# One decoder layer on one core: the sums of the layer input on GpSimd, the rotary key's tile in two passes, the conditioning shared out anew

## The reference, cut to what matters

```python
mod = jax.nn.silu(c) @ w_ada[l] + b_ada[l]
shift, scale, gate = jnp.split(mod[:, None, :], 3, axis=-1)
h = rmsnorm(x, g_pre[l]) * (1.0 + scale) + shift
proj = h @ w_in[l]                      # 1024 x 9920 columns
# c_q 384, c_kv 256, k_pe 64, then gates, retention q, k, v, merge gates
y_mla = mla_branch(c_q, c_kv, k_pe, positions, ...)   # k_pe gets a rotary turn
y_ret = retention_branch(...)
x = x + gate * (merged @ w_out[l])
return rmsnorm(x, g_final)
```

## Time and profile before

| what | us |
|---|---|
| median of 3 runs | 1617.9 |
| the runs | 1614.6, 1617.9, 1619.55 |
| span of the profiled execution | 1616.2 |
| TensorE busy | 1568.4 (97% of the span) |
| VectorE busy | 959.4 (59%) |
| ScalarE busy | 605.1 (37%) |
| GpSimd busy | 322.0 (20%) |

### The profile page before, as it was taken

The page is one execution under the profiler, slowest core; times in us unless marked ns, Lnnn a source line. Parts: engine busy times, 40 slices in busy tenths (PEclk is TensorE's granted clock), DMA queues, the critical chain, the costliest instruction groups (busy, mean ns, idle before and its releaser), DMA issues. The chain is left out here.

```text
span 1616.2 us, 20288 instructions
## 1 busy us (share of the span) xinstructions
PE 1568.4 (97%) x7568; PEld 1308.9 (81%) x7568; DVE 959.4 (59%) x1626; ACT 605.1 (37%) x1057; POOL 322.0 (20%) x280
## 2 busy tenths in 40 slices
PE   5999999999999999999999999899999999999998
PEld 4778888888888888798888888787688888888886
DVE  6984444444444457752566665567987775647544
ACT  5444333333333343342343433334544443213111
POOL 2232223322322200200000000015655530000000
PEclk9999999999999999999999999999999999999999
DMA  9132332223323334799265554447977767345422
GB/s 385 38 130 105 111 112 110 107 109 115 120 104 111 95 97 164 301 414 322 82 209 170 181 184 164 179 137 260 323 235 228 250 204 281 115 137 183 143 105 78
DMA packets 142225, 278.70 MB, mean 172 GB/s; under 512 B 11056, under 2 KB 83632, under 8 KB 133552
## 3 DMA queue, kind: packets, MB, share of 16 engines
q1 hardware_dynamic: 125488, 245.09, 43.6%
q10 hardware_dynamic: 12032, 15.54, 2.9%
q0 software_dynamic: 4608, 16.78, 2.7%
HBM read 182.47 MB, written 94.37 MB: 171 GB/s over the span
## 5 line engine op out<-in xcount | busy, mean ns | idle before, releaser
L1579 DVE TENSOR_TENSOR w_form<-w_pair,w_form 128x512 fp32r<-128x512 f32 x150 | 116.3, 776 | 127.2 <-ACT w_form L1211 125.6
L1211 ACT ACTIVATE w_form<-w_pair 128x512 fp32r<-128x512 f32 x150 | 94.6, 632 | 245.3 <-PE p_banks L2093 237.2
L2090 PE MATMUL p_banks<-h_hi,w_form 128*128 128x512 f32 x300 | 116.8, 389 | 1.1 <-DVE w_form L1579 1.1
L2093 PE MATMUL p_banks<-h_hi,w_form 128*128 128x512 f32 x300 | 116.7, 389 | 0.0
L2092 PE MATMUL p_banks<-h_lo,w_form 128*128 128x512 f32 x300 | 116.7, 389 | 0.0
L1283 ACT ACTIVATE prob<-p_banks,neg_max 128x128 f32<-128x128 f32 (+3 forms) x64 | 47.5, 742 | 182.9 <-DVE neg_max L1693 182.9
L524 ACT ACTIVATE w_hi<-w_raw 128x1024 fp32r<-128x1024 f32 (+2 forms) x69 | 59.5, 866 | 144.9 <-PE p_banks L2348 96.2
L2348 PE MATMUL p_banks<-y_hi,w_lo 128*128 128x512 f32 x256 | 99.6, 389 | 0.0
L2347 PE MATMUL p_banks<-y_lo,w_hi 128*128 128x512 f32 x256 | 99.6, 389 | 0.0
L2346 PE MATMUL p_banks<-y_hi,w_hi 128*128 128x512 f32 x256 | 99.6, 389 | 0.0
L1055 POOL DMA_DIRECT2D v_ret<-v_stage x32 | 17.7, 554 | 410.1 <-DVE v_stage L1670 410.0
(11 more groups left out here) (316 smaller groups left out, 4302.7 us busy)
## 6 DMA issues: line engine op xcount, KB each, us to landing
w_pair<-in_w_pairs SPq DMA_DIRECT2D x25, 1024.0 KB, 4.9
w_raw<-in_w_dense SPq DMA_DIRECT2D x45, 512.0 KB, 4.7
v_ret<-v_stage POOLq DMA_DIRECT2D x32, 512.0 KB, 3.4
v_chunk<-v_ret SPq DMA_DIRECT2D x32, 512.0 KB, 3.7
merge_t<-act_t SPq DMA_DIRECT2D x48, 256.0 KB, 3.4
act_t<-stage SPq DMA_DIRECT2D x40, 256.0 KB, 2.0
act_t<-stage_late SPq DMA_DIRECT2D x40, 256.0 KB, 2.0
ada<-in_w_ada SPq DMA_DIRECT2D x4, 2048.0 KB, 23.9
```

Source lines behind the costliest of these rows:

```text
L1211: self.nc.scalar.activation(self.form[f % FORM_SLOTS][:, 0, :], self.form_source(f), ACT.Copy).then_inc(self.form_hi, 1)
L1579: nc.vector.tensor_tensor(self.form[f % FORM_SLOTS][:, 1, :], self.form_source(f), self.form[f % FORM_SLOTS][:, 0, :].bitcast(F32), ALU.su ...
L2090: self.nc.tensor.matmul(out, w_hi[:, cut], x_hi[:, q, :], start=fresh and q == 0, stop=False, skip_group_check=True)
L2093: last = self.nc.tensor.matmul(out, w_lo[:, cut], x_hi[:, q, :], start=False, stop=q == KD // 2 - 1, skip_group_check=True)
```

## The change

- **Conditioning.** `WEIGHED_ASIDE` says how many of a quarter's eight products VectorE leaves to others: 1, 1, 2, 2. For quarters 2 and 3 GpSimd makes two products and adds them, in place in `ada`. `full` (h_full) goes to ScalarE, behind the two `high` of each quarter. The first weight is rounded by ScalarE instead of VectorE.
- **Rotary key's tile in two passes.** In the second copy of its columns (64 of each 128) the rounded weight is replaced by the low part. One matmul by h_hi and one by h_lo then give high products in one half of the partitions and low products in the other; the L1969 matmul is left out for tile 0. The two halves are exchanged by two transfers into `k_other` and added on VectorE. Only then may the four transfers for `swap` start.
- **Last quarter.** TensorE does all high products of k = 6 and 7 first, then the low products tile by tile. ScalarE rounds tile 3's weight before it evicts tile 0.
- **Sums of h.** GpSimd makes the four `h_sum`, as soon as h_full and h_lo are complete. VectorE's stream keeps the low parts.
- **Angles.** The scratch tiles have other places, since the sums' places are now taken early, and the passes are ordered: three passes of table 1, w_lo of 3, four passes of table 1, w_lo of 4, seven of table 0, the k_other sum, w_lo of 5.

```diff
+WEIGHED_ASIDE = (1, 1, 2, 2)
@@ the places @@
-        self.ang = [z("angle_ret", 16, [P, S]), z("angle_mla", 28, [P, S])]
-        self.turns = [z("turns_ret", 20, [P, S]), z("turns_mla", 56, [P, S])]
+        self.ang = [z("angle_ret", 48, [P, S]), z("angle_mla", 56, [P, S])]
+        self.turns = [z("turns_ret", 44, [P, S]), z("turns_mla", 60, [P, S])]
+        self.k_other = nc.alloc_sbuf_tensor_at("k_pe_other_half", [P, S], F32, offset=stage_at)
@@ lower_weight @@
+        if r == 0:
+            second, raw = (w.rearrange("p (k n) -> p k n", n=P)[:, :, ROPE:P] for w in (self.hi_place(0), self.raw_place(0)))
+            self.nc.vector.tensor_tensor(second, raw, second.bitcast(F32), ALU.subtract).then_inc(self.w_lo_ready, 1)
+            return
@@ sync @@
         sp.wait_ge(self.evicted, 2)
+        for half in range(2):
+            sp.dma_start(self.k_other[ROPE * half:ROPE * (half + 1), :], self.k_pe[ROPE * (1 - half):ROPE * (2 - half), :])\
+                .then_inc(self.swapped, 16)
         sp.wait_ge(self.table, 8)
+        sp.wait_ge(self.roped, 1)
...
@@ gpsimd @@
+            nc.gpsimd.tensor_scalar(first, first, self.silu_c[:, 0:1], None, ALU.mult).then_inc(self.ada_part, 1)
+            if q == 1:
+                return
+            nc.gpsimd.tensor_scalar(second, second, self.silu_c[:, 1:2], None, ALU.mult).then_inc(self.ada_part, 1)
+            pool.wait_ge(self.ada_part, 3 * (q - 1))
+            nc.gpsimd.tensor_tensor(first, first, second, ALU.add).then_inc(self.ada_part, 1)
...
+        pool.wait_ge(self.h_full_ready, KD)
+        pool.wait_ge(self.h_lo_ready, KD)
+        nc.gpsimd.tensor_tensor(self.h_sum[0], h[:, :, 0, 1, :], h[:, :, 0, 0, :], ALU.subtract).then_inc(self.pair_done, 1)
+        nc.gpsimd.tensor_tensor(self.h_sum[2], h[:, :, 1, 1, :], h[:, :, 0, 1, :], ALU.subtract).then_inc(self.pair_done, 1)
+        pool.wait_ge(self.pair_done, 2)
+        nc.gpsimd.tensor_tensor(self.h_sum[1], self.h_sum[2], h[:, :, 0, 0, :], ALU.add).then_inc(self.pair_done, 1)
+        pool.wait_ge(self.pair_done, 3)
+        nc.gpsimd.tensor_tensor(self.h_sum[3], self.h_sum[1], h[:, :, 1, 0, :], ALU.subtract).then_inc(self.pair_done, 1)
@@ scalar @@
+        act.wait_ge(self.w_loaded[0], 16)
+        nc.scalar.activation(self.w_hi[:, 0, :], self.w_raw[:, 0, :], ACT.Copy).then_inc(self.first_w_hi_ready, 1)
...
+        for k in range(2, KD, 2):
             high(k)
+            high(k + 1)
+            full(k)
+            full(k + 1)
         for r in range(R_UP):
+            if r == 0:
+                self.split_weight(act, RING)
             self.evict(act, r)
-            if r < R_UP - RING:
+            if 0 < r < R_UP - RING:
                 self.split_weight(act, r + RING)
@@ vector @@
-        self.angles(dve, 1)
-        for r in range(RING, R_UP):
-            self.lower_weight(dve, r)
-            if r == RING:
-                self.angles(dve, 0)
+        self.whole_turns(dve, 1)
+        self.lower_weight(dve, RING)
+        self.reduced_angles(dve, 1)
+        self.lower_weight(dve, RING + 1)
+        self.whole_turns(dve, 0)
+        self.reduced_angles(dve, 0)
+        dve.wait_ge(self.swapped, 32)
+        nc.vector.tensor_tensor(self.k_pe[:, :], self.k_pe[:, :], self.k_other[:, :], ALU.add).then_inc(self.roped, 1)
+        self.lower_weight(dve, RING + 2)
         dve.wait_ge(self.sines, 2)
-        dve.wait_ge(self.swapped, 64)
+        dve.wait_ge(self.swapped, 96)
...
@@ tensor @@
-                    nc.tensor.matmul(out, w_lo[:, r, cut], h_hi[:, k, tok], start=False, stop=False)
+                    if r:
+                        nc.tensor.matmul(out, w_lo[:, r, cut], h_hi[:, k, tok], start=False, stop=False)
...
+        for k in (6, 7):
+            early_hi(k, range(FIRST))
         for r in range(FIRST):
             for k in (6, 7):
-                early_hi(k, [r])
                 early_lo(k, [r])
```

More of the change, by code:

```diff
@@ L619, in v_stores, with ada_steps @@
         return sum(self.v_slot(n) == self.v_slot(unit) for n in range(unit))
+    def ada_steps(self, q):
+        return sum(KD - aside for aside in WEIGHED_ASIDE[:q])
     def form_bank(self, pair, n):
@@ L969, in weigh @@
         def weigh(q):
-            part = self.stage[:, q % 2, :].rearrange("p (s n) -> p s n", s=2)
+            first, second = (self.ada[:, q, :, k, :] for k in range(2))
             pool.wait_ge(self.ada_loaded[q], 16)
-            if q >= 2:
-                pool.wait_ge(self.ada_step, ADA_STEPS * (q - 1))
             pool.wait_ge(self.silu_ready, 1)
[L976 to L991, removed]
+            nc.gpsimd.tensor_scalar(first, first, self.silu_c[:, 0:1], None, ALU.mult).then_inc(self.ada_part, 1)
[4 more added lines that the diff above has]
+            nc.gpsimd.tensor_tensor(first, first, second, ALU.add).then_inc(self.ada_part, 1)
+        for q in range(1, 4):
+            weigh(q)
+        h = self.h_full
+        pool.wait_ge(self.h_full_ready, KD)
[6 more added lines that the diff above has]
+        nc.gpsimd.tensor_tensor(self.h_sum[3], self.h_sum[1], h[:, :, 1, 0, :], ALU.subtract).then_inc(self.pair_done, 1)
         for pair in range(PAIRS):
@@ L1091, in high, with full @@
                                  scale=self.mod[:, c + 2:c + 3], bias=self.mod[:, c:c + 1]).then_inc(self.h_hi_ready, 1)
+        def full(k):
+            c = 4 * (k // 2) + k % 2
+            nc.scalar.activation(self.h_tile(k), self.x_t[:, k, :], ACT.Identity,
+                                 scale=self.mod[:, c + 2:c + 3], bias=self.mod[:, c:c + 1]).then_inc(self.h_full_ready, 1)
+        act.wait_ge(self.w_loaded[0], 16)
+        nc.scalar.activation(self.w_hi[:, 0, :], self.w_raw[:, 0, :], ACT.Copy).then_inc(self.first_w_hi_ready, 1)
         self.split_weight(act, 1)
@@ L1097, in scalar @@
         self.split_weight(act, 2)
-        for k in range(1, KD):
+        high(1)
+        full(0)
+        full(1)
+        for k in range(2, KD, 2):
             high(k)
+            high(k + 1)
+            full(k)
+            full(k + 1)
         for r in range(R_UP):
+            if r == 0:
+                self.split_weight(act, RING)
             self.evict(act, r)
-            if r < R_UP - RING:
+            if 0 < r < R_UP - RING:
                 self.split_weight(act, r + RING)
@@ L1430, in out_bank, with whole_turns @@
         return MERGE_BANKS[n % 4][half]
-    def angles(self, dve, b):
+    def whole_turns(self, dve, b):
         nc = self.nc
@@ L1447, in angles, with reduced_angles @@
         chained(nc.vector.tensor_scalar(turns, turns, -ROUNDER, None, ALU.add), 3)
+    def reduced_angles(self, dve, b):
+        nc = self.nc
+        ang, turns = self.ang[b][:, :], self.turns[b][:, :]
+        done = 7 * (1 - b)
         for i, part in enumerate((TURN_1, TURN_2, TURN_3)):
-            chained(nc.vector.scalar_tensor_tensor(out=ang, in0=turns, scalar=-part, in1=ang, op0=ALU.mult, op1=ALU.add),
-                    4 + i)
+            nc.vector.scalar_tensor_tensor(out=ang, in0=turns, scalar=-part, in1=ang, op0=ALU.mult, op1=ALU.add)\
+                .then_inc(self.table, 1)
+            dve.wait_ge(self.table, done + 4 + i)
         nc.vector.tensor_scalar(ang, ang, PI_BELOW, -PI_BELOW, ALU.min, ALU.max).then_inc(self.table, 1)
@@ L1495, in weigh @@
             out = self.ada_sum[:, q, :, :]
+            first = WEIGHED_ASIDE[q]
             dve.wait_ge(self.ada_loaded[q], 16)
-            dve.wait_ge(self.ada_part, q) if q else dve.wait_ge(self.silu_ready, 1)
-            for k in range(1, KD):
+            dve.wait_ge(self.ada_part, 3 * q - 2) if q else dve.wait_ge(self.silu_ready, 1)
+            for k in range(first, KD):
                 before = out
@@ L1503, in weigh @@
                     continue
-                if k == 1:
-                    before = self.stage[:, q % 2, :].rearrange("p (s n) -> p s n", s=2)
+                if k == first:
+                    before = self.ada[:, q, :, 0, :]
                 else:
-                    dve.wait_ge(self.ada_step, ADA_STEPS * q + k - 1)
+                    dve.wait_ge(self.ada_step, self.ada_steps(q) + k - first)
                 nc.vector.scalar_tensor_tensor(out=out, in0=self.ada[:, q, :, k, :], scalar=self.silu_c[:, k:k + 1],
```

27 lines of the change are left out of this document (9 added, 18 removed).

## The result

The changed kernel takes 1638.47 us (median of 4 runs, 1635.96 to 1640.26), the kernel before 1617.18 us beside it (1614.6 to 1619.55). The ratio is 1.0123, interval 1.0098 to 1.0148: slower by 1.2%. The forecast was 1637.2. The profiled execution has a span of 1635.1 us, 18.9 above the 1616.2 of before; the sum had given 1635.5.

The account below looks back on a forecast made before the run. VectorE's chain to pair 0 was taken as the bound: pair 0 at 124.8 against 108.3 (+16.5), plus 2.8 us for the clock, gives span 1635.5; the median's 1.7 more gives 1637.2 us, range 1619 to 1641.

Parts of the forecast that it names:

- the clock: TensorE at pair 0: after its wait, 15 matmuls at half clock lose 2.8 us (bounds 0 and twice that).
- The turns: VectorE's angle work: GpSimd's four h sums each block it 4.4 us, 17.6 in all; +19.3 us with clock, chance 0.52.
- Rival 2: VectorE's angle work: fast one-input passes are not blocked by GpSimd's sums; +17.4 us, 1635.3, chance 0.13.
- Rival 3: VectorE's angle-to-key chain: VectorE keeps GpSimd out except at its own waits; +10.7 us, 1628.6, chance 0.10.
- Rival 4: GpSimd's h sums: no blocking at this length, pair 0 at 108.4 plus clock loss; +2.8 us, 1620.7, chance 0.15.
- Rival 5: Ahead of pair 0: VectorE's chain ends before TensorE's, pair 0 at 101.1, no clock loss; -7.2 us, 1610.7, chance 0.07.
- The angles' new places: VectorE's angle scratch tiles at other places: the same operations, costed at nothing.
- The input in PSUM: VectorE beside GpSimd: an operation with an input in PSUM is never stretched (25 times 0.69 us).
- The second exchange: Key's path after the new add: four transfers, 4.3 us together, with only one weight part (1.15 us) covering them.

Follow-up runs that it names:

- the early add: Changed kernel with the h sums on VectorE and the key's two halves added before tile 4's low weight and table 0's angles: 1618.82 us, ratio 1.0011.

## Why the prediction was right

| step | forecast | measured |
|---|---|---|
| TensorE's conditioning sums of quarter 3 begin | 56.3 | 57.0 |
| last low part of h | 63.9 | 64.3 |
| first three tiles end | 67.5 | 68.1 |
| one block of VectorE | 4.4 | 4.27, 4.19, 4.18, 4.36 |
| tile 3 starts | 80.4 | 80.35 |
| key's added sum ends | 98.2 | 97.9 |
| exchange landed | 102.5 | 102.3 |
| key's low part ends | 108.6 | 108.4 |
| store landed | 113.4 | 113.6 |
| pair 0 | 124.8 | 125.15 |
| lost to the clock | 2.8 | 1.3 |
| span | 1635.5 | 1635.1 |

- **The turns.** The step that carried the sum: a GpSimd operation of 2048 elements keeps VectorE out until it ends. The block of 4.4 us was set from two smaller sizes and came within 0.2 us (4.18 to 4.36). How 4.4 follows from 1.0 and 2.25 the prediction doesn't show; a straight line through them gives 4.75, and the 2.25 for 1024 elements was itself a little high: the halved sums block for 2.04 to 2.15. A GpSimd operation of this length was in no row, so part of this closeness is luck.
- **Fast passes.** Rival 2 is out: the passes of 0.69 us at 64.99 and 69.98 last 4.96 and 4.88 us. The rule of the Trainium skill (SBUF — State Buffer, "Who interferes with whom") that one-input passes in the fast mode contend too holds in this trace.
- **Rival 3** (VectorE keeps GpSimd out) is out for this chain: between VectorE's operations of this chain lie gaps of 0.03 us, and GpSimd got its turn in each of the first three; it came in even where VectorE's next operation overlapped the last (80.22 behind 74.89). But the turns are no law without exception. In the kernel before, a GpSimd operation with one input, which takes 1.20 us unhindered, stood from 28.88 while two weight low parts of VectorE passed unstretched (GpSimd, and the second of the two):

```profile
28.88 2.94 POOL L984 TENSOR_SCALAR h_full<-x_t,mod 128x1024 f32<-128x1024 f32 x1
...
29.60 1.22 DVE L530 TENSOR_TENSOR w_lo<-w_raw,w_hi 128x1024 fp32r<-128x1024 f32 x1
```

What decides between the two outcomes no run shows.

- **Rival 4** (no blocking) is out. What it would have given, the run without sums shows: pair 0 at 107.91 against 108.4. **Rival 5** (faster) is out with it: even there TensorE waits 7.30 us for VectorE.
- **The angles' new places** cost nothing, as assumed: with the sums back on VectorE the passes take 0.69 us at the new places.
- **The input in PSUM.** That such VectorE operations are not blocked was read from 25 operations that lie beside GpSimd for 0.4 us at most, mostly for 0.13. Better evidence stands later in the same trace: VectorE's 56 operations that make `state_lo` from PSUM take 0.68 to 0.69 us each, 25 of them wholly beside GpSimd operations that read SBUF.
- **The second exchange** cost its 3.2 us, as the early add shows, but under a blocked VectorE it was not the main thing.
- **Mis-sized:** the clock. I took 2.8 us (15 matmuls) at pair 0; the half-rate stretch had begun during the wait and ended 2.8 us after pair 0's start:

```profile
80.30:83.60 3.30, 3.25 (x8) 2.58 (x9) 3.30 (x1) 0.00 (x0) 3.30 (x1) 0.50 0.00 0
...
125.10:128.00 2.90, 2.85 (x7) 2.29 (x8) 1.07 (x2) 1.13 (x3) 1.59 (x1) 0.50 0.00 0
```

Seven matmuls at about 0.43 instead of 0.227 us, 1.3 us lost. The 18.9 us of the span are then 16.9 at pair 0's start, 1.1 in the paired products (477.6 us against 476.6, the clock's loss) and 0.9 in the later stages. These the change leaves alone, but they take from 1029.2 to 1034.7 us in the twelve traces of this case. So that the span came within 0.4 us of the forecast is partly luck: a clock term 1.5 us too large made up for what was missing elsewhere. The paired products end at 584.8 us in the kernel before, not at about 576; near 576 VectorE's last sum of their outputs begins. The waits of quarter 2 were a little longer than I had it: one GpSimd scaling at 38.97 took 3.06 us, and a low part of h beside it took 1.63.

## What to carry to other kernels

Elementwise work moved from VectorE to GpSimd relieves VectorE where VectorE waits or has an input in PSUM. Against a VectorE that is busy from SBUF it added GpSimd's longer duration to VectorE's own chain (17.0 us here, to save 11.1). Before work is taken off an engine, ask what the next engine waits for: here an operand order (four low parts ahead of a product that needs none) kept TensorE waiting for 6.60 us even with the early stage relieved. Only both together were shown to be faster than before, by 0.24%; how much of that the order brings alone, the timed runs don't tell. A new hop between partitions belongs early in the stream: under angle work the second exchange cost VectorE no wait, behind it 3.2 us.

## What the runs showed of the hardware that I had not expected

- Cutting GpSimd's operations in two left the total block as it was (16.7 and 17.0 us) but spread it: tile 3 gained 6.5 us and tile 4 lost 3.2. The size of the instruction decides who is hit, the elements decide how much.
- How much work falls into the half-rate stretch does not follow from how long TensorE waited: 5.7 us (13 matmuls) after a wait of 7.30 us in the run without sums, 2.9 us (7 matmuls) after 10.36 us at pair 0 of the changed kernel, 3.3 us (8 matmuls) after 12.25 us at its tile 3, and 4.8 us (11 matmuls) after 18.41 us where only the sums were moved. In the changed kernel the clock had fallen during the wait (granted clock 0.50 from 124.0 to 125.1 us, with TensorE idle).
